# First read of the state-space kernel's H rows moved ahead of two G matrices, and two drains on GpSimd, in a two-block transformer kernel

## The chip, the cores and the metric

The program runs on one core of a Trainium2 chip (trn2). Its engines are called here as the profile calls them: PE (TensorE; PEld is its weight load), DVE (VectorE), ACT (ScalarE), POOL (GpSimd), and SP, which here only issues transfers. The metric is the device time of one execution in microseconds (us), the median of several runs. Lower is better.

## What is computed

Two transformer blocks in a row on 512 tokens of width 1024, all in float32. Block one: a mixer (convolution and dilated attention), cross-attention to 256 memory rows with 4 heads of 256, and a mixture of 32 experts with two per token. Block two: a forgetting attention and a state-space layer (S5) side by side, and again 32 experts, half as wide.

What the change touches is the preparation of the state-space layer of block two, which depends on parameters alone:

```python
A_bar = jnp.exp(A * dt)
B_bar = ((A_bar - 1.0) / A)[..., None] * Bm
Bu = jnp.einsum('bsgc,gpc->bsgp', uf.astype(jnp.complex64), B_bar)
A_seq = jnp.broadcast_to(A_bar, Bu.shape)
_, state = lax.associative_scan(_linear_combine, (A_seq, Bu), axis=1)
Cm = lax.complex(C_re.astype(f32), C_im.astype(f32))
y = jnp.real(jnp.einsum('gcp,bsgp->bsgc', Cm, state))
```

The kernel runs the recurrence in chunks of 8 tokens with matrices made beforehand: G (powers of A_bar times B_bar, into the state), H (C times powers of A_bar, out of the state), and K = B_bar by H, the response inside a chunk, written to DRAM as the triangular matrices T.

## The kernel before

One instruction stream per engine is written out by hand, and semaphores tie them. An engine works strictly in the order written; a `wait_ge` holds everything behind it on its engine.

The stages around the change, by their place in the profiled execution:

- Until about 405 us POOL computes eight H pieces (`s5_matrices_pool`, L1157 to L1166) and writes them to the DRAM tensor `ssm_h` (L1171). Beside this PE works on block one.
- POOL then makes four G matrix pieces (u = 0 to 3, L1185 to L1199), each followed by `g_ready` + 1. DVE makes the other four (`s5_late_dve`, L1229 to L1236), each followed by `g_late` + 1. POOL's temporaries `G_tmp` lie in `work[:, 2048:3072]`, DVE's in `work[:, 1024:2048]`.
- After its four pieces POOL reads H rows back for the K product: for each quad q = 0 to 3 two transfers (L1209) into `Hq`, which lies over both of those temporaries, `work[:, 1024:3072]`. Hence the first read stands behind all of POOL's pieces and behind `g_late` 4. The read for q waits for `k_done` q, the K product before it.
- PE meanwhile computes the queries of the cross-attention (L278) and enters its loop over 16 (head, tile) pairs (`xattn_pe`). In each pass it does scores (L278), four transposes of one G piece (`s5_turn_pe`, L1247) and the transposes of the probabilities (L1316). In every fourth pass (n = 3, 7, 11, 15) it waits for the H rows (`hq_in`) and does the K product of quad n // 4: 8 matmuls, 16 in the profile (L1256); then come the matmuls by the values (L278). In these passes PE's later work stands behind `hq_in`.
- Passes 0 to 3 use the G pieces u = 0 and 1, passes 4 to 7 u = 2 and 3 (POOL's), passes 8 to 15 DVE's.
- DVE copies each K product into `KS` (L1270, L1271), in `work[:, 5120:6144]`, where B_bar and C, which POOL's G pieces read, lie too. Once all four stand there, POOL writes T (L1213).
- SP loads the first two expert matrices when the queries no longer need their places, and waits for T to be written (`t_out`, L2143) before the third.

Then come block one's output projection and experts, the entry of block two (`entry_pool` on POOL, L2386), the state-space layer, attention, and the second expert stage. There `moe_pool` (m = 9) adds each expert's rows into the output with an indirect transfer (L2095): for expert e it waits for `yready`; the buffer `yb` has four places, so ACT's scaling for expert e (L2022) waits for the add of expert e - 4 to have landed.

```python
pool.wait_ge(S("g_late"), 4)
pool.wait_ge(S("tab_out"), 32)
for q in range(4):
    if q:
        pool.wait_ge(S("k_done"), q)
    for c in range(2):
        pool.dma_start(Hq[:, :, c, :], by_quad(Hm)[:, q, :, 288 * c:288 * c + 256]).then_inc(S("hq_in"), 16)
```

Of the kernel before, what the change touches and what calls it, by code (L numbers as in the profile page):

```python
# [190 lines left out]
def build(nc, a, out):  # L191
    es = ExitStack()
    with es:
# [13 lines left out]
        def since(name):  # L207

            return SHARED.get(name, (name, 0))[1]
# [798 lines left out]
        G_tmp = work[:, 2048:3072].rearrange("p (a f e n) -> p a f e n", a=4, f=2, e=8)  # L1008
        G_tmp_late = work[:, 1024:2048].rearrange("p (a f e n) -> p a f e n", a=4, f=2, e=8)
        B_tmp = spare[:, 5376:6400].rearrange("p (a i n) -> p a i n", a=4, n=16)  # L1010
        Hq = work[:, 1024:3072].rearrange("p (f c n) -> p f c n", f=4, c=2)
        KS = work[:, 5120:6144].rearrange("p (q n) -> p q n", q=4)

        def G_of(n):
# [104 lines left out]
        def s5_matrices_pool(pool):  # L1119
            done = [0]  # L1120

            def op(ins):
                ins.then_inc(S("pool_chain"), 1)
                done[0] += 1

            def settle():
                pool.wait_ge(S("pool_chain"), done[0])

            tt = nc.gpsimd.tensor_tensor
            halves = (slice(0, 64), slice(64, P))  # L1130
            after_stage(pool, 2)
            pool.dma_start(raw_bc, a["ssm_bc"]).then_inc(S("bc_in"), 16)
            op(nc.gpsimd.memset(spare[:, 3072:5376], 0.0))
            op(nc.gpsimd.memset(spare[:, 7168:8192], 0.0))
            pool.wait_ge(S("sp_done"), 1)
            pool.wait_ge(S("bc_in"), 16)
            kr, ki = (sc[:, i, :].unsqueeze(2).to_broadcast([P, SS, 16]) for i in (12, 13))
            op(tt(B_tmp[:, 0], B_bar[:, 0], kr, ALU.mult))
            op(tt(B_tmp[:, 1], B_bar[:, 1], ki, ALU.mult))
            op(tt(B_tmp[:, 2], B_bar[:, 1], kr, ALU.mult))  # L1140
            op(tt(B_tmp[:, 3], B_bar[:, 0], ki, ALU.mult))
            settle()
            op(tt(B_bar[:, 0], B_tmp[:, 0], B_tmp[:, 1], ALU.subtract))
            op(tt(B_bar[:, 1], B_tmp[:, 2], B_tmp[:, 3], ALU.add))
            settle()
            for c in range(2):
                for h, r in enumerate(halves):
                    op(nc.gpsimd.tensor_copy(B_mask[r, c, :, h, :], B_bar[r, c]))
            settle()
            for u in range(8):  # L1150
                Q, f0 = u // 2, 2 * (u % 2)
                sh = [P, 2, 9, 16]
                cr, ci = (by_quad(C_raw[:, c])[:, Q, f0:f0 + 2, :].unsqueeze(2).to_broadcast(sh) for c in range(2))
                are, nai = (w.rearrange("p e (f q) -> p q f e", q=4)[:, Q, f0:f0 + 2, :].unsqueeze(3).to_broadcast(sh)
                            for w in (pw[:, 0], nim))
                settle()
                op(tt(H_tmp[:, 0], cr, are, ALU.mult))  # L1157
                op(tt(H_tmp[:, 1], ci, nai, ALU.mult))
                op(tt(H_tmp[:, 2], cr, nai, ALU.mult))
                op(tt(H_tmp[:, 3], ci, are, ALU.mult))  # L1160
                settle()
                if u >= 2:
                    pool.wait_ge(S(f"h_out{u % 2}"), 16 * (u // 2))
                for h, r in enumerate(halves):
                    op(tt(H_buf[r, u % 2, :, 0, :, h, :], H_tmp[r, 0], H_tmp[r, 1], ALU.add))
                    op(tt(H_buf[r, u % 2, :, 1, :, h, :], H_tmp[r, 2], H_tmp[r, 3], ALU.subtract))  # L1166
                    if u == 0 and h == 0:
                        resnorm_pool("n5", 0, 1)
                        pool.wait_ge(S("n5_rstd"), since("n5_rstd") + 1)
                settle()  # L1170
                pool.dma_start(by_quad(Hm)[:, Q, f0:f0 + 2, :],  # L1171
                               spare[:, 3072 + 1152 * (u % 2):4224 + 1152 * (u % 2)].rearrange("p (f n) -> p f n", f=2)
                               ).then_inc(S(f"h_out{u % 2}"), 16)
                if 1 <= u < T:
                    resnorm_pool("n5", u, u + 1)
                if u == T:
                    pool.wait_ge(S("tab_sin"), 2)
                    pool.dma_start(Km[:, 0:2 * SS * CH], work[:, 0:2 * SS * CH]).then_inc(S("tab_out"), 16)
                    pool.dma_start(Km[:, 2 * SS * CH:3 * SS * CH], junk2[:, :]).then_inc(S("tab_out"), 16)

            for b in range(2):
                pool.wait_ge(S(f"h_out{b}"), 16 * 4)
            for u in range(4):
                Q, f0 = u // 2, 2 * (u % 2)
                op(nc.gpsimd.memset(spare[:, 3072 + 1024 * u:4096 + 1024 * u], 0.0))  # L1185
                sh = [P, 2, 8, 16]
                br, bi = (by_quad(B_bar[:, c])[:, Q, f0:f0 + 2, :].unsqueeze(2).to_broadcast(sh) for c in range(2))
                are, aim = (prv[:, c].rearrange("p e (f q) -> p q f e", q=4)[:, Q, f0:f0 + 2, :].unsqueeze(3).to_broadcast(sh)
                            for c in range(2))
                settle()  # L1190
                op(tt(G_tmp[:, 0], br, are, ALU.mult))
                op(tt(G_tmp[:, 1], bi, aim, ALU.mult))
                op(tt(G_tmp[:, 2], br, aim, ALU.mult))
                op(tt(G_tmp[:, 3], bi, are, ALU.mult))
                settle()
                area = spare[:, 3072 + 1024 * u:4096 + 1024 * u].rearrange("p (f c e h n) -> p f c e h n", f=2, c=2, e=8, h=2)
                for h, r in enumerate(halves):
                    op(tt(area[r, :, 0, :, h, :], G_tmp[r, 0], G_tmp[r, 1], ALU.subtract))
                    op(tt(area[r, :, 1, :, h, :], G_tmp[r, 2], G_tmp[r, 3], ALU.add))  # L1199
                settle()  # L1200
                pool.sem_inc(S("g_ready"), 1)

            pool.wait_ge(S("g_late"), 4)
            pool.wait_ge(S("tab_out"), 32)
            for q in range(4):
                if q:
                    pool.wait_ge(S("k_done"), q)
                for c in range(2):
                    pool.dma_start(Hq[:, :, c, :], by_quad(Hm)[:, q, :, 288 * c:288 * c + 256]).then_inc(S("hq_in"), 16)  # L1209
            pool.wait_ge(S("ks_ready"), 8)  # L1210
            pool.wait_ge(S("zeroed"), 16 * (STEPS - 1))
            for s in range(STEPS):
                pool.dma_start(Tm[s // 2, :, :, s % 2, 32 * s:256], KS[:, :, 0:256 - 32 * s]).then_inc(S("t_out"), 16)  # L1213
# [25 lines left out]
        def s5_turn_pe(pe, n):  # L1239
            if n < 8:  # L1240
                pe.wait_ge(S("g_ready"), n // 2 + 1)
            else:
                pe.wait_ge(S("g_late"), n // 2 - 3)
            if n:
                pe.wait_ge(S("gt_out"), n)
            for b in range(4):
                last = nc.tensor.transpose(ps[:, 6, b * P:b * P + P], G_of(n)[:, b * P:b * P + P], ident[:, :])  # L1247
            last.then_inc(S("gt_turned"), 1)
            if n % 4 == 3:
                q = n // 4  # L1250
                pe.wait_ge(S("hq_in"), 32 * (q + 1))
                if q:
                    pe.wait_ge(S("ks_ready"), 2 * q)
                for f in range(4):
                    for c in range(2):
                        last = nc.tensor.matmul(ps[32 * f:32 * f + 32, 7, 0:256],  # L1256
                                                B_mask[:, c, q + 4 * f, :, :].rearrange("p h n -> p (h n)"),
                                                Hq[:, f, c, :], start=c == 0, stop=c == 1)
                last.then_inc(S("k_done"), 1)

        def s5_turned_act(act, n):
# [5 lines left out]

        def s5_kernel_dve(dve, q):
            dve.wait_ge(S("k_done"), q + 1)
            dve.tensor_copy(KS[:, q, 32:256], ps[:, 7, 32:256]).then_inc(S("ks_ready"), 1)  # L1270
            dve.scalar_tensor_tensor(KS[:, q, 0:32], col("eye32", 0, 32), col("ssm_d", q), ps[:, 7, 0:32], ALU.mult,  # L1271
                                     ALU.add).then_inc(S("ks_ready"), 1)
# [790 lines left out]
        def moe_pool(pool, m):  # L2063
# [13 lines left out]
            for e in range(NE):  # L2077
# [3 lines left out]
                add_rows(pool, m, rowdst[:, expert(e):expert(e) + 1], yb[:, e % 4, :]).then_inc(S(f"yadd{m}_{e % NG}"), 16)  # L2081
                if e % 2 == 1 and e // 2 + 4 < NE // 2:
                    gather(e // 2 + 4)
                if e == NE - 8:
                    pool.wait_ge(S(f"planned{m}"), since(f"planned{m}") + 1)
                    pool.wait_ge(S(f"xturned{m}"), since(f"xturned{m}") + NE // 2 - 3)
# [1030 lines left out]
        def _(pool):  # L3117
# [4 lines left out]
            moe_pool(pool, 6)  # L3122
            over_pool(pool, 6)
            entry_pool(pool)
            fox_in_pool(pool)
            fox_pool(pool)
            mix2_pool(pool)
# [103 lines left out]
```

## Time and profile before

| | |
|---|---|
| median of 3 runs | 1804.73 us (1803.51 to 1806.19) |
| the profiled execution: time, span | 1803.88 us, 1802.0 us |
| busy: PE, DVE, ACT, POOL | 89%, 30%, 18%, 22% of the span |
| moved by DMA | 437.16 MB, mean 243 GB/s |
| mean granted TensorE clock | 0.978 of full speed |

The span runs from the first to the last instruction of the profiled execution; its time has 1.88 us more around it. A busy PE is not a PE at its peak, and the share of busy time is an average over stages with different limits. In rows of the profile, [x <-y] is the idle time before an instruction and what ended it; L12 is line 12 of the kernel before. The two expert stages (about 576 to 1054 us and 1535 to 1790 us) stream 32 experts' weights each; between them lies block two's mixer.

### The profile page before, as it was taken

What the parts mean: (1) busy time and instruction counts of PE and PEld (TensorE: products, weight loads), DVE (VectorE), ACT (ScalarE), POOL (GpSimd) and SP (SyncE); (2) the same over time, 40 slices, a digit from 0 to 9 for tenths busy, and PEclk for the clock granted to TensorE, in tenths of its full rate; (3) what the DMA queues carried; (4) which work ended last, traced back from release to release, by engine and by line L of the source; (5) the groups of instructions that cost most, each with busy time, mean ns of one, the idle gap of its engine ahead of it and who ended that gap; (6) DMA issues with size and microseconds to landing.
All of it is one profiled execution on the core that took longest, in us unless ns stands there. A gap on an engine that the chain in (4) does not pass through costs nothing.

```text
span 1802.0 us, 22881 instructions
## 1 busy us (share of the span) xinstructions
PE 1598.7 (89%) x9029; PEld 873.0 (48%) x9029; DVE 539.2 (30%) x1227; ACT 331.9 (18%) x710; POOL 392.2 (22%) x377
## 2 busy tenths in 40 slices
PE   7999999997998999777877759999999998899885
PEld 4445666443545554333343326444444444667553
DVE  3765554742315221001010022614400015321110
ACT  3002453221312000000000030413510003111110
POOL 0121442686101111111111110014201000223222
PEclk9999999999998999999999989999999999999998
DMA  8343111253466999999999977921041265999995
GB/s 310 101 128 118 47 48 59 73 207 140 163 245 232 395 415 414 419 420 415 418 420 418 414 229 210 268 96 47 1 86 56 92 247 208 346 398 397 399 403 202
DMA packets 103480, 437.16 MB, mean 243 GB/s; under 512 B 16249, under 2 KB 23961, under 8 KB 77137
## 3 DMA queue, kind: packets, MB, share of 16 engines
q1 hardware_dynamic: 75888, 387.12, 55.4%
q0 software_dynamic: 18320, 30.76, 6.3%
q10 hardware_dynamic: 9168, 17.84, 2.7%
q8 instruction: 73, 1.20, 0.3%
q14 instruction: 31, 0.25, 0.0%
HBM read 410.98 MB, written 40.65 MB: 251 GB/s over the span
## 4 chain that ended last, share of the span: by engine, by line
PE 58%; DMA 27%; POOL 5%; DVE 4%; issue 2%; ACT 2%; SPq 1%; ACTq 0%; POOLq 0%; DVEq 0%
PE ps L278 23%; DMA ring<-in_w 19%; PE ps L1928 9%; PE ps L1461 5%; DMA ring<-in_w_expert_up 4%; PE ps L1944 4%; PE ps L756 2%; PE ps L2446 2%; PE ps L1447 2%; DMA ring<-in_w_expert_down 1%; PE ps L811 1%; PE ps L844 1%; PE ps L2955 1%; PE ps L761 1%; PE ps L859 1%
## 5 line engine op out<-in xcount | busy, mean ns | idle before, releaser
L1928 PE MATMUL ps<-ring,work 128*64 128x256 f32 (+1 forms) x2784 | 252.5, 330 | 41.7 <-DMA ring<-in_w 29.2
L278 PE MATMUL ps<-kept,ring 128*128 128x512 f32 x592 | 256.1, 593 | 4.3 <-ACT kept L542 1.3
L1928 PEld LDWEIGHTS ps<-ring,work 128*64 128x64 f32 x2784 | 172.4, 137 | 127.1 <-DMA ring<-in_w 48.1
L278 PEld LDWEIGHTS ps<-kept,ring 128*128 128x128 f32 x592 | 111.8, 190 | 145.9 <-issue 142.0
L2056 DVE TENSOR_TENSOR work<-work,ps 128x256 f32<-128x256 f32 (+1 forms) x64 | 22.7, 355 | 496.9 <-PE ps L1928 496.9
L1944 PE MATMUL ps<-ring,work 128*64 128x512 f32 x536 | 125.5, 603 | 32.5 <-DMA ring<-in_w 25.1
L2095 POOL DMA_INDIRECT hres<-work,rowdst x33 | 51.7, 1567 | 403.9 <-ACT work L2022 389.6
L1928 PE MATMUL ps<-kept,work 128*64 128x256 f32 (+1 forms) x1280 | 116.4, 330 | 20.7 <-DMA kept<-in_w 14.8
L278 PE MATMUL ps<-ring,kept 128*128 128x512 f32 (+1 forms) x320 | 125.1, 550 | 0.6 <-PE ps L278 0.6
L1928 PEld LDWEIGHTS ps<-kept,work 128*64 128x64 f32 x1280 | 80.1, 137 | 60.7 <-DMA kept<-in_w 23.5
L2012 ACT ACTIVATE work<-ps 128x256 f32<-128x256 f32 (+1 forms) x64 | 21.1, 330 | 438.5 <-PE ps L1928 438.5
L278 PEld LDWEIGHTS ps<-ring,kept 128*128 128x128 f32 x320 | 60.3, 190 | 63.0 <-issue 61.0
L2095 POOL DMA_INDIRECT out<-work,rowdst x33 | 51.8, 1570 | 171.1 <-ACT work L2022 170.8
L1461 PE MATMUL ps<-ring,kept 128*128 128x512 f32 x192 | 85.2, 595 | 1.0 <-ACTq L257 0.7
L2022 ACT ACTIVATE work<-ps,gslot 128x512 f32<-128x512 f32 x64 | 44.0, 687 | 211.8 <-PE ps L1944 211.8
L1944 PEld LDWEIGHTS ps<-ring,work 128*64 128x64 f32 x536 | 36.7, 138 | 94.4 <-issue 58.1
L1944 PE MATMUL ps<-kept,work 128*64 128x512 f32 x240 | 58.5, 624 | 14.5 <-DMA kept<-in_w 9.5
L1461 PE MATMUL ps<-ring,work 128*128 128x512 f32 x128 | 58.6, 611 | 2.4 <-POOL work L3018 2.2
L1461 PEld LDWEIGHTS ps<-ring,kept 128*128 128x128 f32 x192 | 35.4, 190 | 43.5 <-issue 41.9
L278 PE MATMUL ps<-ring 128*128 128x512 f32 x128 | 55.3, 592 | 0.0
L647 DVE SCALAR_TENSOR_TENSOR ring<-ring,cols 128x512 f32<-128x512 f32 x60 | 54.5, 950 | 0.6
L3011 DVE TENSOR_TENSOR work<-work,ps 128x512 f32<-128x512 f32 x16 | 11.0, 689 | 136.3 <-PE ps L278 136.3
(470 smaller groups left out, 1973.6 us busy)
## 6 DMA issues: line engine op xcount, KB each, us to landing
ring<-in_w SPq DMA_DIRECT2D x65, 2048.0 KB, 42.0
kept<-in_w SPq DMA_DIRECT2D x28, 2048.0 KB, 42.5
ring<-in_w_in SPq DMA_DIRECT2D x13, 2048.0 KB, 14.7
ring<-in_w_expert_down SPq DMA_DIRECT2D x23, 1024.0 KB, 23.4
ring<-in_w_expert_gate SPq DMA_DIRECT2D x22, 1024.0 KB, 20.6
ring<-in_w_expert_up SPq DMA_DIRECT2D x22, 1024.0 KB, 22.4
kept<-in_w_expert_gate SPq DMA_DIRECT2D x10, 1024.0 KB, 23.4
kept<-in_w_expert_down SPq DMA_DIRECT2D x10, 1024.0 KB, 23.9
```

What stands on the lines that cost most here:

```text
L278: last = nc.tensor.matmul(out_, l, r, start=i == 0, stop=i == len(pairs) - 1)
L647: ins = dve.scalar_tensor_tensor(cacc[:, c, :], cpad[:, c, j:j + SEQ], w, cacc[:, c, :], ALU.mult, ALU.add)
L756: last = nc.tensor.matmul(dst.rearrange("p (m n) -> p m n", m=MT), weight(f"w_xk{u // 4}")[:, k, u % 4 * P:u % 4 * P + P], memT[:, :, k, : ...
L1447: last = nc.tensor.matmul(ps[:, t, :], src(k)[:, t * P:t * P + P], weight(nm)[:, k, :], start=k == 2, stop=k == 1)
L1461: last = nc.tensor.matmul(ps[:, b * T + t, :], src(k)[:, t * P:t * P + P], weight(nm)[:, k, :], start=k == 0, stop=k == KD - 1)
L1928: last = nc.tensor.matmul(dst[64 * hf:64 * hf + 64, :], xT[:, k, :], view[:, k * ff + hf * hw:k * ff + hf * hw + hw], start=k == 0, stop=k ...
L1944: last = nc.tensor.matmul(ps[64 * hf:64 * hf + 64, bank, :], hT_[:, i % nch, 64 * (i // nch):64 * (i // nch) + 64], down[:, i, hf * 512:hf ...
L2012: nc.scalar.activation(gb[:, i % 2, 0:hw], ps[:, 0, 0:hw], ACT.Silu).then_inc(S(f"silu{m}"), 1)
L2022: nc.scalar.activation(yb[:, j % 4, :], ps[:, 6 + j % 2, :], ACT.Identity, scale=gslot[:, expert(j):expert(j) + 1]).then_inc(S(f"yready{m} ...
L2056: dve.tensor_tensor(hb[:, i % 2, 0:hw], gb[:, i % 2, 0:hw], ps[:, 1, 0:hw], ALU.mult).then_inc(S(f"hready{m}"), 1)
L2095: return pool.indirect_dma_start(out=by_half(acc(m)), out_offset=bass.IndirectOffsetOnAxis(ap=rows_, axis=0), in_=src, in_offset=None, bou ...
L2446: last = nc.tensor.matmul(ps[64 * q:64 * q + 64, s2, :], hs[:, k, 2 * s2 + q, :], weight("u")[:, k, :], start=k == 0, stop=k == KD - 1)
```

## The change

The H rows get two other places, one for each half c: `spare[:, 1024:2048]` (inside the tile `ring`) and `work[:, 1024:2048]`. The read for q = 0 is issued behind POOL's second G piece (u = 1), ahead of the third and fourth, after waits for `n5_turned`, `g_late` 4 and `tab_out`. The other reads stay behind all four pieces and behind `k_done`. DVE's copy of the first K product waits for `g_ready` 4 besides. POOL gets two `drain()` instructions: one after `entry_pool`, before `fox_in_pool`; one in the second expert stage behind the add of expert 22 (`NE - 10`).

```diff
-        Hq = work[:, 1024:3072].rearrange("p (f c n) -> p f c n", f=4, c=2)
+        Hq = [v.rearrange("p (f n) -> p f n", f=4) for v in (spare[:, 1024:2048], work[:, 1024:2048])]
...
+            def h_rows(q):
+                if not q:
+                    pool.wait_ge(S("n5_turned"), since("n5_turned") + T)
+                    pool.wait_ge(S("g_late"), 4)
+                    pool.wait_ge(S("tab_out"), 32)
+                for c in range(2):
+                    pool.dma_start(Hq[c], by_quad(Hm)[:, q, :, 288 * c:288 * c + 256]).then_inc(S("hq_in"), 16)
...
                 pool.sem_inc(S("g_ready"), 1)
-
-            pool.wait_ge(S("g_late"), 4)
-            pool.wait_ge(S("tab_out"), 32)
-            for q in range(4):
-                if q:
-                    pool.wait_ge(S("k_done"), q)
-                for c in range(2):
-                    pool.dma_start(Hq[:, :, c, :], by_quad(Hm)[:, q, :, 288 * c:288 * c + 256]).then_inc(S("hq_in"), 16)
+                if u == 1:
+                    h_rows(0)
+
+            for q in range(1, 4):
+                pool.wait_ge(S("k_done"), q)
+                h_rows(q)
...
-                                                Hq[:, f, c, :], start=c == 0, stop=c == 1)
+                                                Hq[c][:, f, :], start=c == 0, stop=c == 1)
...
             dve.wait_ge(S("k_done"), q + 1)
+            if not q:
+                dve.wait_ge(S("g_ready"), 4)
...
+                if e == NE - 10 and m == 9:
+                    pool.drain()
...
             entry_pool(pool)
+            pool.drain()
             fox_in_pool(pool)
```

On POOL, at the end of the second G piece, the order before (`ring<-work` are the G pieces, `ssm_h` the H rows in DRAM; waits are named by semaphore):

```order
L1198 TENSOR_TENSOR ring<-work 64x2x8x16
L1199 TENSOR_TENSOR ring<-work 64x2x8x16
L1185 MEMSET ring 128x1024 [waits pool_chain]
L1191 TENSOR_TENSOR work<-work 128x256 [waits pool_chain]
L1192 TENSOR_TENSOR work<-work 128x256
```

and now:

```order
L1206 TENSOR_TENSOR ring<-work 64x2x8x16
L1207 TENSOR_TENSOR ring<-work 64x2x8x16
L1187 DMA ring<-ssm_h 128x4x256 [waits pool_chain,tab_out,g_late,norm_turned]
L1187 DMA work<-ssm_h 128x4x256
L1193 MEMSET ring 128x1024
L1199 TENSOR_TENSOR work<-work 128x256 [waits pool_chain]
L1200 TENSOR_TENSOR work<-work 128x256
```

Two transfers and their waits have come in between the second and the third piece.

On POOL behind the fourth G piece, before:

```order
L1209 DMA work<-ssm_h 128x4x256 [waits pool_chain,tab_out,g_late]
L1209 DMA work<-ssm_h 128x4x256
L1209 DMA work<-ssm_h 128x4x256 [waits k_done]
L1209 DMA work<-ssm_h 128x4x256
L1209 DMA work<-ssm_h 128x4x256 [waits k_done]
L1209 DMA work<-ssm_h 128x4x256
```

and now:

```order
L1187 DMA ring<-ssm_h 128x4x256 [waits pool_chain,k_done]
L1187 DMA work<-ssm_h 128x4x256
L1187 DMA ring<-ssm_h 128x4x256 [waits k_done]
L1187 DMA work<-ssm_h 128x4x256
L1187 DMA ring<-ssm_h 128x4x256 [waits k_done]
L1187 DMA work<-ssm_h 128x4x256
```

The first pair is gone from here; the pairs for q = 1 to 3 are the same transfers at the same place, each half into its own tile.

## Rows read from the trace of the kernel before

**Rows 1.** the page: shares of the chain that ended last, by engine

```profile
PE 58%; DMA 27%; POOL 5%; DVE 4%; issue 2%; ACT 2%; SPq 1%; ACTq 0%; POOLq 0%; DVEq 0%
```

**Rows 2.** the chain in order of time, 400 to 500 us: start, us, what

```profile
433.51 0.80 POOL work L1209
434.31 15.29 DMA work<-ssm_h
```

**Rows 3.** timeline of PE, 440 to 490 us: start, us, what, idle before

```profile
440.55 0.63 PE L1247 MATMUL ps<-ident,ring 128*128 128x128 f32 x4 [0.16 <-ACT ring L1264]
449.65 1.96 PE L1256 MATMUL ps<-work,ring 128*32 128x256 f32 x16 [8.47 <-DMA work<-ssm_h]
...
463.89 1.09 PE L1256 MATMUL ps<-work,ring 128*32 128x256 f32 x16
...
476.16 1.09 PE L1256 MATMUL ps<-work,ring 128*32 128x256 f32 x16
```

**Rows 4.** windows: length; busy PE, PEld, DVE, ACT, POOL; clock, DMA share, GB/s

```profile
420.00:432.00 12.00, 12.00 (x29) 5.13 (x27) 0.00 (x0) 0.60 (x1) 11.38 (x17) 1.00 0.00 0
...
446.00:448.00 2.00, 0.00 (x0) 0.00 (x0) 0.00 (x0) 0.00 (x0) 0.00 (x0) 0.50 0.90 279
```

**Rows 5.** timeline of POOL, 380 to 490 us

```profile
418.95 0.72 POOL L1199 TENSOR_TENSOR ring<-work 64x256 f32<-64x256 f32 x1
...
426.42 0.95 POOL L1185 MEMSET ring<- 128x1024 f32 x1 [0.15 <-POOL ring L1199]
...
432.13 0.73 POOL L1199 TENSOR_TENSOR ring<-work 64x256 f32<-64x256 f32 x1
433.51 1.56 POOL L1209 DMA_DIRECT2D work<-ssm_h  x2 [0.66 <-POOL ring L1199]
```

**Rows 6.** timeline of DVE, 414 to 450 us

```profile
414.11 0.89 DVE L1236 TENSOR_TENSOR kept<-work 64x256 f32<-64x256 f32 x1
```

**Rows 7.** H reads issued after 450 us, then all after 430 us

```profile
DMA to landing us min/median/max: 4.3/4.8/5.4
...
DMA to landing us min/median/max: 4.3/8.5/15.3
```

**Rows 8.** DMA issues, 430 to 434 us: count, KB each, us to landing

```profile
ring<-in_w SPq DMA_DIRECT2D x2, 2048.0 KB, 15.7
work<-ssm_h POOLq DMA_DIRECT2D x1, 512.0 KB, 12.1
```

**Rows 9.** timeline of SP's issues, 420 to 760 us

```profile
432.34 0.81 SPq L2123 DMA_DIRECT2D ring<-in_w  x2
502.07 0.33 SPq L2123 DMA_DIRECT2D work<-in_w  x1
502.49 55.92 SPq L2123 DMA_DIRECT2D ring<-in_w  x4
```

**Rows 10.** SP's waits, 432 to 600 us: total, times, longest

```profile
SPq L2143 <- DMA ssm_t<-work: 68.8, 1, 68.8
```

**Rows 11.** windows, around and in the first expert stage

```profile
540.00:560.00 20.00, 19.04 (x99) 10.15 (x99) 11.03 (x41) 6.90 (x16) 1.36 (x3) 1.00 0.31 114
...
600.00:660.00 60.00, 58.01 (x436) 33.12 (x433) 14.77 (x41) 5.68 (x11) 10.05 (x7) 1.00 1.02 410
```

**Rows 12.** timeline of POOL, entry of block two and second expert stage

```profile
1191.73 5.43 POOL L2796 TENSOR_TENSOR qstat<-qstat,halves 128x32 f32<-128x32 f32 x1 [118.39 <-DVE qstat L2782]
...
1705.50 1.58 POOL L2095 DMA_INDIRECT out<-work,rowdst  x1 [5.51 <-ACT work L2022]
1715.52 1.56 POOL L2095 DMA_INDIRECT out<-work,rowdst  x1 [8.45 <-ACT work L2022]
```

**Rows 13.** timeline of ACT, the scaling for expert 27

```profile
1747.01 0.69 ACT L2022 ACTIVATE work<-ps,gslot 128x512 f32<-128x512 f32 x1 [1.78 <-PE ps L1944]
```

**Rows 14.** DMA issues of the span: the adds, median us to landing

```profile
out<-work,rowdst POOLq DMA_INDIRECT x33, 8.5
```

**Rows 15.** window late in the second expert stage

```profile
1660.00:1780.00 120.00, 98.00 (x1137) 66.38 (x1135) 16.74 (x37) 14.87 (x30) 31.57 (x24) 1.00 1.02 397
```

## The prediction

> **What bounds the kernel now.** I read the shares of the chain first: PE carries 58% of it, transfers 27% [rows 1]. PE is the bound of most stages, and a wait on PE is time of the kernel if everything behind it follows PE. So I looked at the place of the change in the chain in order of time. Ahead of the first K product it does not run through PE at all but through POOL, piece by piece: the issue of the first H rows at 433.51, then 15.29 us of transfer [rows 2]. The timeline of PE shows the other end: PE finishes its fourth G transpose at 440.55 + 0.63 = 441.2, sits idle 8.47 us for the H rows, and starts the K product at 449.65 [rows 3]. The windows show the clock: 1.00, that is 2.4 GHz, in 420 to 432 us, where PE is busy without a break, and 0.50, that is 1.2 GHz, in 446 to 448 us, five us into the idle time [rows 4]. So the first K product takes 1.96 us and the later ones 1.09 [rows 3].
>
> **Part 1, the first H read moves up.** The second G piece of POOL ends at 418.95 + 0.72 = 419.7 us [rows 5]. The moved read waits for three things. The last of DVE's late G pieces ends at 414.11 + 0.89 = 415.0 [rows 6], 4.7 us before POOL asks. `n5_turned` and `tab_out` are what DVE's memset ahead of those pieces waits for too, so both are older still. The two transfers are thus issued from 419.7 to about 421.9. In 420 to 432 us the DMA engines are idle, share 0.00 [rows 4]. The six later H reads land in 4.3 to 5.4 us [rows 7], so I take 5.4: the rows are there by 427.3, 13.9 us before PE asks at 441.2. The 8.47 us are gone.
>
> The clock follows. From K product to K product PE takes 463.89 - 449.65 = 14.24 us in the first round and 476.16 - 463.89 = 12.27 us in the second [rows 3]; both rounds hold the same work. The difference, 1.97 us, is what the low clock cost the first round. Without the idle time nothing in these rows makes PE slower than in the second round, whose rhythm of small gaps ran at 1.00. Saved: 8.47 + 1.97 = 10.44 us. If the clock stayed low for another reason, 8.47 would be left; it can't give more than both.
>
> **Part 2, what stands behind the read on POOL.** The issues of a pair take 1.56 us plus 0.66 us of gap [rows 5]. The third G piece now ends at 426.42 + 2.2 = 428.6, the fourth at 432.13 + 0.73 + 2.2 = 435.1. PE needs the third in its fifth pass, behind the first K product, so after 442.3: 13.7 us of cover. The new wait of DVE's first `KS` copy on `g_ready` 4 is for 435.1, and that copy also waits for the K product at 442.3; behind it on DVE stand the copies of the probabilities, which PE awaits, and they are not held. Both parts cost 0. If the cover went, POOL would have to be 7 us later than reckoned.
>
> **Part 3, the second H read meets the weights.** What is late next is the read for q = 1. It is issued behind the K product, at 441.2 + 1.09 = 442.3, into the transfer of two expert matrices, 4 MB, that SP issued at 432.34. Those took 15.7 us to land, and the first pair of H rows, issued 1.2 and 2 us behind them, 12.1 and 15.3 [rows 8] [rows 7]. In the changed kernel the same bytes are under way up to 450 us: the matrices, one pair of H rows (now q = 1), the G pieces of ACT. All of them had landed at 434.31 + 15.29 = 449.6 [rows 2]. PE asks for q = 1 one round behind the first product, at 441.2 + 12.3 = 453.5. That leaves 3.9 us; I count 0. Whether the read shares or queues is the open point. The rows show sharing: the pair issued behind the matrices landed about with them. The Trainium skill, "DMA: Bandwidth & Descriptors", section "Queues, rings and completion order", says that each transfer engine takes turns between its queues packet by packet. By that rule the read would not stand behind what is left of the matrices; the sum would be the same, and rival A would be rarer than the rows alone make it.
>
> **Part 4, does the saving reach the end?** SP issued its third expert load at 502.07 and the next from 502.49 [rows 9], and it had waited 68.8 us for T to be written [rows 10]. T follows the fourth K product, so this load moves up with PE. The others wait for PE's output projection. In 540 to 560 us the transfers are at a share of 0.31, from 600 us at 1.02 [rows 11]: the saturated stream begins behind work that is itself 10.4 us earlier, and only the two matrices of 432 us, which had landed by 448 us, are not tied to it. The entry of block two, the mixer and the second expert stage each wait for the one before. I pass on all of it.
>
> **Part 5, the drains.** No row shows a drain on POOL. The one at the entry falls into 118.39 us in which POOL is idle [rows 12]; between 0 and 118 us it costs nothing. The one in the second expert stage stands behind the add for expert 22, which ends at 1705.50 + 1.58 = 1707.1; the next add starts at 1715.52 after 8.45 us of idle time [rows 12]. Up to 8.4 us it delays nobody. Beyond that the add for expert 23 is late, which ACT awaits before it scales expert 27, at 1747.01 [rows 13]; the add needs 8.5 us to land [rows 14]. So the drain may last 1747.0 - 8.5 - 1707.1 = 31.4 us before it costs anything. The bounds are 0 and the end of the stage's stream: the DMA share is 1.02 until 1780 us [rows 15], 72.9 us. Nearest to a drain is the issue that it follows, 1.58 us, and I take 0 for the end. A drain frees nothing that another engine awaits, so no gain either. The Trainium skill, "PSUM — Partial Sum Buffer", section "Engine vs sequencer instructions", has a drain wait until its engine is fully idle; by this rule it ends with POOL's own work and the cost is also 0, while a drain that waited for the transfers it had issued would still stay under 31.4.
>
> **The sum.** 10.44 saved and 0 added: the profiled execution's 1803.88 us would be 1793.4. The median of the runs shown is 0.85 above that execution, so the forecast is 1804.73 - 10.44 = **1794.3 us**.
>
> **The rivals.**
> A, a new wait in place of the old: the read for q = 1 takes 15.3 us as its forerunner did, from its second issue at 443.1, and lands at 458.4. PE waits 4.9 us, and the clock falls as before for up to 1.97. Saved 3.6 to 5.5, say 4.2: 1800.5. For it speaks that the load on the queues at the issue is nearly the same; against it that by then 10 of the 15.7 us of the matrices are over. 6%.
> B, the gain is swallowed by the first expert stage, which streams 400 us at the limit of the transfers. 1804.7. It would need the stream's start to be fixed in time; the wait of 68.8 us on T speaks against it. 5%.
> C, slower: the drain in the second expert stage holds POOL until the transfers under way have landed, in a stage in which they don't cease before 1780 us. It costs nothing up to 31.4 us and outweighs the saving from 31.4 + 10.4 = 41.8 us on. At its full 72.9 us it delays expert 27 by 41.5 us: 1794.3 + 41.5 = 1835.8. Against it: the nearest rows of POOL are in single microseconds. 3%.
> D, the change does not do what it says: one of the three waits holds POOL, the read goes out as late as before, and third and fourth G pieces stand behind it. 1804.7. The 4.7 us of margin on `g_late` speak against it. 2%.
>
> **How the numbers follow.** The forecast has the other 84%. A measurement of this kernel can tell about 0.2%, 3.6 us, from no change. Faster: forecast and A, 0.90. Within it: B and D, 0.07. Slower: C, 0.03. The range: at the low end the fastest run shown less the saving, 1803.51 - 10.44, less the 2.7 us by which the runs shown differ, 1790.4; at the high end rival A, 1800.5. It takes in the 8.47 without the clock (1796.3) and leaves out 10%.
>
> **What the profile after would show.** Right: the first pair of H reads issued near 420 us and landed by 428; no idle time of PE for `ssm_h` before the first K product, which starts at about 441.2 and takes 1.1 us; a clock of 1.00 in 442 to 456 us; four K products 12.3 us apart; SP's third expert load at 491.6; the same 10.4 us at every later landmark; POOL's adds from expert 23 on not later than ACT's scalings. Wrong: PE idle for H rows before the second product (A); that load 10 us earlier and the end of the first expert stage not (B); a gap on POOL behind the add for expert 22 that ends at no scaling (C); the first H pair near 433 us (D).

## The result and the profile after

The changed kernel takes **1788.24 us** (median of 4 runs, 1787.69 to 1791.32); the kernel before took 1804.12 us beside it (4 runs, 1803.15 to 1806.19). The ratio is 0.9911, 95% interval 0.9899 to 0.9923: 16 us faster, where 10.4 were forecast. 1788.24 lies 2.2 us below the range, 1790.4 to 1800.5. The profiled execution of the changed kernel took 1791.32 us, its span is 1789.5.

The chain of the page, by engine, against [rows 1]:

```profile
PE 62%; DMA 26%; DVE 4%; ACT 2%; issue 2%; POOL 2%; SPq 1%; ACTq 0%; POOLq 0%; DVEq 0%
```

POOL has fallen from 5% to 2% of it and PE risen from 58% to 62%: ahead of the first K product the chain now runs through PE, as the timelines show.

The first part went as reckoned. The timeline of POOL in the changed kernel, around the moved read (start, us, what, idle before):

```profile
420.34 0.73 POOL L1207 TENSOR_TENSOR ring<-work 64x256 f32<-64x256 f32 x1
421.75 0.80 POOL L1187 DMA_DIRECT2D ring<-ssm_h  x1 [0.69 <-POOL ring L1207]
422.55 0.75 POOL L1187 DMA_DIRECT2D work<-ssm_h  x1
...
435.64 0.73 POOL L1207 TENSOR_TENSOR ring<-work 64x256 f32<-64x256 f32 x1
443.96 0.78 POOL L1187 DMA_DIRECT2D ring<-ssm_h  x1 [7.58 <-PE ps L1262]
```

The first pair of H rows goes out at 421.75, not 433.51 [rows 5]; the profiled execution as a whole is 1.4 us later here than the one before, and was so ahead of the change (PE's passes begin at 434.33 where they began at 432.93). The pair for q = 1 waits 7.58 us for the first K product and for nothing else. The issues of 419 to 423 us, us to landing:

```profile
ring<-ssm_h POOLq DMA_DIRECT2D x1, 512.0 KB, 4.4
work<-ssm_h POOLq DMA_DIRECT2D x1, 512.0 KB, 5.7
```

The second of the pair, issued at 422.55, is there by 428.3. PE's timeline:

```profile
441.95 0.63 PE L1253 MATMUL ps<-ident,ring 128*128 128x128 f32 x4 [0.16 <-ACT ring L1270]
442.51 0.66 PE L1262 MATMUL ps<-ring 128*32 128x256 f32 x8
442.96 0.64 PE L1262 MATMUL ps<-work,ring 128*32 128x256 f32 x8
...
454.78 0.66 PE L1262 MATMUL ps<-ring 128*32 128x256 f32 x8
...
467.06 0.66 PE L1262 MATMUL ps<-ring 128*32 128x256 f32 x8
...
479.34 0.66 PE L1262 MATMUL ps<-ring 128*32 128x256 f32 x8
```

No idle time stands ahead of the first K product, where there were 8.47 us [rows 3]. The products are 12.27, 12.28 and 12.28 us apart. The clock is 1.00 (2.4 GHz) where it had been 0.50 [rows 4]:

```profile
442.00:456.00 14.00, 12.87 (x86) 8.30 (x87) 6.61 (x22) 6.40 (x17) 1.54 (x2) 1.00 0.83 304
446.00:448.00 2.00, 1.03 (x4) 0.44 (x3) 1.56 (x6) 0.74 (x2) 0.00 (x0) 1.00 0.80 293
```

SP's third expert load stood at 502.07 [rows 9] and is now 9.17 us earlier, 10.6 against the start of PE's passes:

```profile
492.90 0.33 SPq L2133 DMA_DIRECT2D work<-in_w  x1
```

The other 5 to 6 us come from a place that the forecast does not have. The last transfer that POOL issues adds the rows of the overflow round to the output. Timeline of POOL, the kernel before (span 1802.0):

```profile
1788.39 1.58 POOL L2095 DMA_INDIRECT out<-work,tokcol  x1 [5.49 <-ACT work L2234]
```

and the changed kernel (span 1789.5):

```profile
1781.48 1.58 POOL L2105 DMA_INDIRECT out<-work,tokcol  x1 [5.48 <-ACT work L2244]
```

The add comes 6.91 us earlier, the end of the span 12.5. From the end of that add to the end of the span, called the tail from here on, it was 12.03 us and is now 6.44. (Spans are printed to a tenth, so every tail below is good to 0.05 us.) No timeline has an instruction of POOL in that stretch, since timelines leave control instructions out. The view of one line has them: line 193 is the end of the program. The kernel before, first (durations in ns min/median/max, first and last start in us):

```profile
L193 POOLq DRAIN  x1: 6814/6814/6814, 1795.0 to 1795.0; - x1
L193 SPq DRAIN  x1: 13/13/13, 1768.4 to 1768.4; - x1
L193 ACTq DRAIN  x1: 8/8/8, 1795.4 to 1795.4; - x1
L193 DVEq DRAIN  x1: 10/10/10, 1795.4 to 1795.4; - x1
L193 PEldq DRAIN  x1: 8/8/8, 1795.5 to 1795.5; - x1
```

The changed kernel:

```profile
L193 POOLq DRAIN  x1: 1200/1200/1200, 1788.1 to 1788.1; - x1
L193 SPq DRAIN  x1: 13/13/13, 1761.5 to 1761.5; - x1
L193 ACTq DRAIN  x1: 8/8/8, 1788.5 to 1788.5; - x1
L193 DVEq DRAIN  x1: 66/66/66, 1788.8 to 1788.8; - x1
L193 PEldq DRAIN  x1: 8/8/8, 1788.6 to 1788.6; - x1
```

Every engine closes with a drain that the source does not write. POOL's took 6.81 us and is the last thing that happens but for 0.2 us of semaphores; now it takes 1.20. The difference, 5.61 us, is the whole of what the tail lost (5.59). The added drains themselves, the entry's and the expert stage's:

```profile
L3135 POOLq DRAIN  x1: 6017/6017/6017, 1066.0 to 1066.0; - x1
L2093 POOLq DRAIN  x1: 10696/10696/10696, 1698.3 to 1698.3; - x1
```

They are not short: 6.02 and 10.70 us. The first runs out at 1072.0, long before POOL's next operation, and the second ends at 1709.0. Timeline of POOL behind the first and around the second, against [rows 12]:

```profile
1184.89 5.43 POOL L2806 TENSOR_TENSOR qstat<-qstat,halves 128x32 f32<-128x32 f32 x1 [118.16 <-DVE qstat L2792]
...
1698.54 1.58 POOL L2105 DMA_INDIRECT out<-work,rowdst  x1 [5.53 <-ACT work L2030]
1710.19 1.56 POOL L2105 DMA_INDIRECT out<-work,rowdst  x1 [10.07 <-PE ps L1927]
1715.76 1.60 POOL L2105 DMA_INDIRECT out<-work,rowdst  x1 [2.63 <-ACT work L2030]
```

and of ACT, the scaling for expert 27, against [rows 13]:

```profile
1740.06 0.69 ACT L2030 ACTIVATE work<-ps,gslot 128x512 f32<-128x512 f32 x1 [1.81 <-PE ps L1952]
```

### The profile page after: what moved, and what is told of

It reads as the page before. It is cut to its first block, busy times and chain, and to the rows that moved or that the text cites. A ratio compares the mean times of both kernels' runs of the same rounds, so it can differ in the third digit from the quotient of the medians.

```text
span 1789.5 us, 22884 instructions
## 1 busy us (share of the span) xinstructions
PE 1600.4 (89%) x9029; PEld 875.2 (49%) x9029; DVE 539.4 (30%) x1227; ACT 331.9 (19%) x710; POOL 391.5 (22%) x377
## 4 chain that ended last, share of the span: by engine, by line
PE 62%; DMA 26%; DVE 4%; ACT 2%; issue 2%; POOL 2%; SPq 1%; ACTq 0%; POOLq 0%; DVEq 0%
PE ps L278 27%; DMA ring<-in_w 19%; PE ps L1936 9%; PE ps L1469 5%; DMA ring<-in_w_expert_up 4%; PE ps L1952 4%; PE ps L756 2%; PE ps L2456 2%; PE ps L761 2%; PE ps L1455 2%; DMA ring<-in_w_expert_down 1%; PE ps L811 1%; PE ps L844 1%; PE ps L2965 1%; PE ps L859 1%
## 5 line engine op out<-in xcount | busy, mean ns | idle before, releaser
L1952 PE MATMUL ps<-ring,work 128*64 128x512 f32 x536 | 129.2, 618 | 33.1 <-DMA ring<-in_w 25.0
L1952 PE MATMUL ps<-kept,work 128*64 128x512 f32 x240 | 55.5, 597 | 14.7 <-DMA kept<-in_w 10.4
```

The costliest lines, as they stand in the source:

```text
L1952: last = nc.tensor.matmul(ps[64 * hf:64 * hf + 64, bank, :], hT_[:, i % nch, 64 * (i // nch):64 * (i // nch) + 64], down[:, i, hf * 512:hf ...
```

## The experiments

The first four were made when the closing drain had not been looked at; what was known was that the saving was 6 us too large and that it sat behind the last add.

**The read alone.** The change without both drains.

```diff
-                if e == NE - 10 and m == 9:
-                    pool.drain()
...
-            pool.drain()
```

> The moved H read without either drain. Seen so far: the changed kernel is 15.9 us faster by its median, 12.5 by its span; in the profile the stretch from the end of POOL's last add to the end of the span is 12.0 us before and 6.4 after, and an instruction fetch falls into it before. Theory P (place in the code: the drains move the last instructions of POOL against the blocks in which its code is fetched): 10.4 us faster than before, tail of 12.0 us as before. Theory R (the extra 5.5 us belong to the moved read or to chance in the transfer-bound stages; the drains do nothing): 16 us faster, tail of 6.4. Theory Q (a drain does something where it stands): 10.4, and the tail could be either.

Measured: 1794.66 us (1791.92 to 1795.69, 5 runs), ratio 0.9941, interval 0.9928 to 0.9954. Against the 1805.54 of the kernel before beside it that is 10.9 us, and against the forecast 1794.3 it is 0.4 off. The tail is 12.06 us, as before. What was forecast is what the read does.

**The drains alone.** The kernel before with both drains.

```diff
+                if e == NE - 10 and m == 9:
+                    pool.drain()
...
+            pool.drain()
```

> The kernel before with both drains and the H read where it was. P: 5.6 us faster than before, tail of 6.4 us, the 8.5 us wait of PE for the H rows unchanged. R: no difference, tail of 12.0. Q: 5.6 us faster, and the time is gained near 1707 us, behind the drain, not in the tail.

Measured: 1801.45 us (1797.36 to 1803.35, 7 runs), ratio 0.9971, interval 0.996 to 0.9983, so 5.2 us faster by the ratio and 4.1 by the medians: clear of no change. The tail is 6.44 us, that of the change, though the last add of its profiled execution comes at 1793.48, later than before. PE still waits 8.32 us for the H rows. The shares add up, 0.9941 times 0.9971 is 0.9912. Theory R is out.

**The read and one drain,** first the one at the entry, then the one in the expert stage.

```diff
             entry_pool(pool)
+            pool.drain()
```

> Moved read and the drain at the entry of block two alone. P: this drain and the other are worth the same, one instruction each: e3 and e4 come out alike, both 10.4 us faster than before if one instruction is too little to move the end, both 16 if one suffices. Q: 10.4, if the drain of the expert stage is the one that counts. R: 16.

```diff
+                if e == NE - 10 and m == 9:
+                    pool.drain()
```

> Moved read and the drain in expert stage two alone. P: the same as e3. Q: 16 us faster, unlike e3. R: 16.

Measured: entry 1793.0 us (1789.39 to 1795.15, 6 runs), ratio 0.9931, interval 0.9919 to 0.9943, tail 9.62 us; expert stage 1788.7 us (1787.13 to 1789.59, 5 runs), ratio 0.9906, interval 0.9893 to 0.9919, tail 6.41. One drain is as good as two if it is the later one, and the earlier gives less than half. That is neither Theory P, by which the two are alike, nor Theory Q, whose gain would lie right behind the drain. In the view of line 193 the closing drains are:

```profile
L193 POOLq DRAIN  x1: 4397/4397/4397, 1785.5 to 1785.5; - x1
```

```profile
L193 POOLq DRAIN  x1: 1201/1201/1201, 1786.3 to 1786.3; - x1
```

Counted in the trace, 132 transfers of POOL stand ahead of the closing drain in the kernel before, 53 behind the entry drain, 14 behind that of the expert stage. (The record of that drain begins 0.2 us ahead of the row of the add that stands before it in the program; counted by start times this add falls behind the drain. The expectations below count so: 15 behind that drain, 39 with 24 more transfers, 38 ahead of it, and 14 up to a drain in the overflow round. In the order of the program it is 14, 38, 39 and 13.) 4.40 / 53 = 0.083 and 1.20 / 14 = 0.086 us. Hence a new theory, B: a drain works off what POOL's transfers have left behind since the last one. Its rival is again the place of the code.

With the expert-stage drain alone 118 transfers stand ahead of it, and it takes 12.79 us instead of 10.70; the kernel is no slower for that.

**Two drains at the entry.**

```diff
             entry_pool(pool)
             pool.drain()
+            pool.drain()
```

with the one in the expert stage left out.

> The read as in the change, both drains in a row at the entry of block two, none in expert stage two: as many POOL instructions ahead of the end as in the change. What the records of the closing drain (line 193, POOL) show so far: 6.81 us without an added drain (132 POOL transfers issued since the start), 4.40 us with the entry drain alone (53 issued since), 1.20 us in both kernels with the expert-stage drain (15 issued since). Theory B, backlog: POOL's closing drain works off what its transfers left behind since its last drain, about 0.083 us for each. Then the second entry drain takes under 0.2 us, the closing one 4.40, and the stretch from the last add's end to the end of the span is 9.6 us. Theory P, place: what counts is where the closing code lies, so how many instructions stand ahead of it. Then two drains at the entry do what the two of the change do: closing drain 1.2 us, stretch 6.4.

Measured: 1793.08 us (one run), tail 9.67.

```profile
L3133 POOLq DRAIN  x1: 6017/6017/6017, 1065.5 to 1065.5; - x1
```

```profile
L3134 POOLq DRAIN  x1: 47/47/47, 1071.5 to 1071.5; - x1
```

```profile
L193 POOLq DRAIN  x1: 4391/4391/4391, 1786.6 to 1786.6; - x1
```

Theory P falls: two drains at the entry leave the closing drain where one leaves it. The second, right behind the first, costs 0.047 us, so an instruction of this kind is not long in itself.

**More transfers behind the last drain.**

```diff
                 if e == NE - 10 and m == 9:
                     pool.drain()
+                if e >= NE - 8 and m == 9:
+                    for i in range(3):
+                        at = 16 * (3 * (e - NE + 8) + i)
+                        pool.dma_start(Gm[:, at:at + 16], ident[:, 0:16]).then_inc(S("filler"), 16)
+                    pool.wait_ge(S("filler"), 48 * (e - NE + 9))
```

> The change, and behind each of the last eight adds of expert stage two three more small transfers issued by POOL (128 rows of 16 numbers into a scratch tensor that nothing reads), 24 in all, behind the last drain. Theory B, backlog: 15 + 24 = 39 transfers stand behind the last drain, so the closing drain takes 39 * 0.083 = 3.2 us instead of 1.20, and the stretch behind the last add is 8.5 us. If only indirect transfers count it stays at 1.20. Theory P, place: anything, without relation to the count.

```profile
L193 POOLq DRAIN  x1: 3160/3160/3160, 1799.9 to 1799.9; - x1
```

3.16 us for 38 transfers. The 24 more cost 1.96 us, 0.082 each: the forecast of 3.2 holds, and plain transfers count like indirect ones. (Both kinds have 128 rows here, so these runs don't tell whether transfers or their rows are counted.) The tail is 7.97, less than the 8.5 expected, since POOL was at its closing drain 4.6 us behind the last add and not 5.0. The kernel itself takes 1805.13 us (one run): the wait for the three fillers holds POOL about 8 us behind each of the first five adds and 2 us behind the last three, which is the edit's doing and no matter here.

**More compute behind the last drain.** The same with small copies.

```diff
+                if e >= NE - 8 and m == 9:
+                    for i in range(3):
+                        at = 16 * (3 * (e - NE + 8) + i)
+                        nc.gpsimd.tensor_copy(junk[:, at:at + 16], ident[:, 0:16])
```

> The change, and behind each of the last eight adds of expert stage two three small POOL copies (128 by 16 numbers into a scratch tile) in place of the three transfers of the run before: 24 more compute instructions behind the last drain. Theory B as the last runs left it (closing drain = 0.081 us for each POOL transfer since the last drain: 15 give 1.20, 39 gave 3.16, 53 gave 4.40): compute leaves nothing behind, the closing drain stays at 1.20 us and the stretch behind the last add at 6.4. Theory C, every POOL instruction leaves something: it grows, to as much as 3.2 us.

Measured: closing drain 1.200 us, tail 6.47, 1789.32 us (one run). Transfers alone leave something behind. Theory C falls.

**Is there a cap?** The read alone, with the 24 fillers, no drain.

> The read of the change, no added drain, and the 24 more transfers of the run with more transfers: 156 POOL transfers stand behind no drain but the closing one, where 132 took 6.81 us. Theory B with a cap (132 at 0.083 would be 10.9, not 6.81; 79 took 6.02): what a drain works off is bounded, the closing drain takes 6.81 us again. Theory B without a cap, with cheaper transfers of the first block: 24 more at 0.081 make it 8.8 us.

```profile
L193 POOLq DRAIN  x1: 6814/6814/6814, 1795.9 to 1795.9; - x1
```

156 transfers take what 132 took, to the nanosecond (the kernel takes 1804.79 us, one run, with the waits for the fillers in it). So what a drain works off is bounded, and the bound is reached by 132. With 79 it was 6.02 (the entry drain), which is 0.5 less than 79 times 0.082: either the bend begins below 79, or block one's transfers, other ones than these, cost less. Nor do these runs show what is full.

**What does a drain cost that nothing covers?** One behind every add of expert stage two.

```diff
-                if e == NE - 10 and m == 9:
+                if m == 9:
                     pool.drain()
```

> The change with its expert-stage drain made 32: one behind every expert's add in stage two. It prices a drain that nothing covers. In the change that one drain's record is 10.70 us long, begins with the add ahead of it, and the next add is issued 11.65 us after the one before, against 9.10 us in the kernel with the entry drain alone. 38 transfers at 0.083 us are 3.2 us of it. Theory B, backlog alone: each of the 32 drains has 1 or 2 transfers behind it, so a record of under 2 us (the add's own 1.6 us in it), adds come as far apart as before (5.5 to 9 us), and the time stays within 1 us of the change's, with a closing drain of 1.20. Theory L, a drain also waits until POOL's transfers in flight have landed (8.5 us for an add): each record is 8 to 10 us long, adds are at least 9 to 10 us apart instead of 6.2 us on average in the first 20, and the kernel is 40 to 90 us slower.

Measured: 1843.71 us (1840.86 to 1845.38, 4 runs), ratio 1.0216, interval 1.02 to 1.0231, 55 us slower than the change. The view of the drain's line, and POOL's timeline:

```profile
L2093 POOLq DRAIN  x32: 3527/8082/14321, 1545.3 to 1826.6; - x32
```

```profile
1641.28 1.56 POOL L2105 DMA_INDIRECT out<-work,rowdst  x1 [8.52 <-ACT work L2030]
1643.15 1.06 POOL L2078 DMA_INDIRECT work<-hmid,rowtok  x1 [0.30 <-issue]
1653.24 1.58 POOL L2105 DMA_INDIRECT out<-work,rowdst  x1 [9.03 <-issue]
1664.03 1.56 POOL L2105 DMA_INDIRECT out<-work,rowdst  x1 [9.21 <-ACT work L2030]
```

With one or two transfers ahead of it a drain still takes 8.08 us in the median, while the adds that this kernel issues up to 1790 us take 8.3 us from issue to landing. The landings themselves show what it waits for. One drain begins at 1653.02 and ends at 1663.18; the add, issued at 1653.24, landed 9.87 us later, at 1663.11. The views of the two lines at that place, the drain first:

```profile
L2093 POOLq DRAIN  x1: 10162/10162/10162, 1653.0 to 1653.0; - x1
```

```profile
DMA to landing us min/median/max: 9.9/9.9/9.9
```

The one before stands behind an add and a gather; the gather, issued at 1643.15, landed at 1652.27 and the drain ended at 1652.38, 2.9 us behind the add's landing. Of the 32 drains, 31 end 0.07 to 0.12 us behind the landing of the last transfer ahead of them, the first 0.30 us. From the first add to the twentieth it is 200.3 us (1545.56 to 1745.87) instead of 127.7 (1545.83 to 1673.55) in the change, where adds are 6.7 us apart and not 6.2 as the expectation has it. The closing drain takes 0.216 us here, with two transfers behind the last of the 32 (the 1.20 of the expectation belongs to 14). So a drain does two things: it works off the backlog, and it waits until POOL's transfers in flight have landed. How the two go together is open: the drain behind expert 22 in the change ends 1.65 us behind the landing of its add, neither 0.07 nor the 3.2 of 39 transfers. Theory L holds, and with it the mechanism of rival C; only its price was wrong, since one drain waits for POOL's own transfers and not for SP's stream.

**A third drain,** in the overflow round, where POOL waits 5.48 us for the last scaled rows.

```diff
+                    if m == 9:
+                        pool.drain()
                     pool.wait_ge(S(f"over{m}_yready"), b + 2)
```

> The change with a third drain: in the overflow round of expert stage two, behind the gather and ahead of POOL's wait for the last scaled rows, where POOL sits idle for 5.48 us. Theory B, backlog: one transfer is issued behind it, so the closing drain falls from 1.20 us to about 0.1, and the stretch behind the last add from 6.44 to 5.3 to 5.4 us; the third drain itself has 14 transfers to work off (about 1.2 us, or until the gather just issued has landed, 2.2 us) and stays inside the idle time, so the kernel is 1.1 us faster than the change. Theory L, a drain also waits for the transfers in flight: the same, as only the gather is in flight. Theory P, place: one more instruction, no forecast below 1.2 us. If the last add is issued later than in the change by more than 0.3 us against the last gather, the drain was not covered.

Measured: 1789.6 us (1786.57 to 1790.99, 5 runs), ratio 0.9916, interval 0.9903 to 0.993. The third drain takes 1.61 us and is covered, since the last add is issued 6.56 us behind the last gather, where it was 6.55. The closing drain falls as said, but the tail only to 6.15 us, not to 5.3:

```profile
L193 POOLq DRAIN  x1: 123/123/123, 1786.3 to 1786.3; - x1
L193 DVEq DRAIN  x1: 66/66/66, 1787.1 to 1787.1; - x1
```

POOL is done at 1786.4 and the span ends at 1787.4: between them stand the closing steps of the other engines, DVE's last. They begin when ACT and PE have stepped through their own skipped rounds of the overflow loop; in the change ACT's last one ends at 1788.15, as POOL comes to its closing drain (1788.1):

```profile
L2235 ACTq COMPARE_BRANCH  x30: 40/45/54, 1046.3 to 1788.1; - x30
```

So 0.3 us of the 1.08 come out, too little for the measurement.

**The entry and the overflow drain,** without the one in the expert stage, and **the change again** beside it.

> The read of the change, the drain at the entry of block two, and the third drain of the earlier run (overflow round of expert stage two, ahead of POOL's wait for the last scaled rows), without the drain behind expert 22. The overflow drain has 52 transfers to work off, 52 * 0.083 = 4.3 us, in an idle time of 5.48 us, so it is just covered. The closing drain is 0.12 us and the stretch behind the last add 6.15 us, 0.3 less than in the change. The drain behind expert 22 put the next add 11.65 us behind its predecessor against 9.10: if that late add costs something (from the first load of expert stage two to the last add: 338.4, 339.0 and 339.4 us with that drain and the read, 337.1, 337.7 and 337.8 without), this kernel gives it back: 1 to 1.5 us faster than the change in all. If the late add costs nothing: 0.3 us faster, which 5 rounds cannot tell from none. If the overflow drain is not covered, the last add comes more than 6.56 us behind the last gather.

> The change as it is, again, for the runs beside it: ratio to the kernel before 0.991, expert drain 10.7 us, closing drain 1.20, stretch behind the last add 6.44. From the first load of expert stage two to the last add: 338.4 us if the scatter of that stage is small, 337 to 339.5 if it is as large as the runs so far allow.

Measured: 1790.38 us (1789.27 to 1790.87, 4 runs), ratio 0.9912, interval 0.9895 to 0.9928, and the change 1788.77 (1787.2 to 1789.4, 4 runs), ratio 0.9902, interval 0.9886 to 0.9919. The change has 10.58 and 1.20 us in its expert-stage and closing drains and a tail of 6.4, as expected. In the other kernel the overflow drain takes 4.32 us for 52 transfers, the last add is issued 6.57 us behind the last gather, the tail is 6.10. From the first load of expert stage two to the last add this kernel takes 339.2 us, the change this time 337.6 and the first time 338.4. The same kernel differs by 0.8 us from one time to the next, and the one without the late add takes longest. So the 1 to 1.5 us that the late add seemed to cost are not seen. Of all kernels tried none beats the change; with the expert-stage drain alone (1788.7) it is as fast.

## Why the prediction was wrong

**Part 1** is right to a tenth: no idle time ahead of the first K product, a clock of 1.00, and the last K product at 479.34 where it stood at 488.44, 9.1 us and the 1.4 of the late start: 10.5 us against 10.44. Moved alone, the read gives 10.6 us by the ratio and 10.9 by the medians.

**Part 2** holds. The fourth G piece ends at 435.64 + 0.73 = 436.4 us, ahead of the first K product (442.5), so neither the copy of DVE nor PE waits for it.

**Part 3** holds, with less room than reckoned. The q = 1 pair, issued at 443.96 and 444.74, landed 7.6 and 8.7 us later:

```profile
ring<-ssm_h POOLq DMA_DIRECT2D x1, 512.0 KB, 7.6
work<-ssm_h POOLq DMA_DIRECT2D x1, 512.0 KB, 8.7
```

That is 453.4, and PE asks at 454.8. Rival A, with 15.3 us, did not come. The margin was 1.4 us and not the 3.9 that I gave it: the rows came later than 449.6, the time that I took from the kernel before. The packets show why. There the first packet of the pair moved at 437.87, 4.4 us behind the issue, and from then on its packets went between those of the matrices, whose last began at 447.90: the two shared. Now the first packet of the q = 1 pair moves at 448.28, 4.3 us behind the issue, and the matrices' last begins at 447.86: nothing was left to share, and the changed kernel does not test the sharing that I reckoned with. The q = 0 pair, issued at 421.75 while the transfer engines were idle, had its first packet after 1.5 us. What holds the first packet back in the other two cases is open.

**Part 4** holds within what one execution can say. The 9.17 us at SP's third load are 6.91 at the last add of the first profiled execution and 8.86 at that of the second (1779.53). The first expert stage gives and takes some 2 us from one execution to the next (from that load to the reading back of `hres` it is 555.8 us in the kernel before and 555.4 to 558.0 in the twelve executions with the read); by the medians nothing is lost. Rival B is out, and D too. That the two profiled executions differ by 12.5 us where the medians differ by 15.9 is this scatter.

**Part 5 failed,** with the sentence "A drain frees nothing that another engine awaits, so no gain either", and ahead of it with "No row shows a drain on POOL". One did: the closing drain, 6814 ns, in the view of line 193. I had looked for the end of the kernel in timelines, where the last row of POOL was at 1788.39 in a span of 1802.0, and did not ask what the 12.03 us behind it were. What a drain saves is work of a later drain, and the last one of POOL lies at the end of the program with nothing beside it. The term that the sum put at nothing is 6.81 - 1.20 = 5.61 us; with it the forecast would be 1794.29 - 5.61 = 1788.7 us, against 1788.24 measured.

The same part was wrong on the length as well. I took the row of an issue, 1.58 us, as nearest; the drain behind expert 22 is 10.70 us long. Its next add is issued 11.65 us behind its predecessor, where with the entry drain alone it is 9.10. It cost nothing all the same, for the reason given there: ACT needs that add only for expert 27, whose scaling starts at 1740.06, 21 us after the add had landed (1718.85). Of the rule I had cited from the Trainium skill, "PSUM — Partial Sum Buffer", section "Engine vs sequencer instructions", that a drain waits for its engine to go fully idle, the traces show that for POOL idle takes in its transfers: in the run with 32 drains they end when the last transfer ahead of them has landed.

The Trainium skill, "VectorE: DVE Perf Modes", section "The DRAIN you can't avoid", calls the drains that the runtime puts around a program about 12 ns long on all five engines. For SP, ACT, DVE and PE the trace of the kernel before about agrees (13, 8, 10 and 8 ns; in the changed kernel DVE's is 66). For POOL it is 6814 ns with 132 transfers ahead of it; here the measurement decides.

## What to carry to other kernels

Look at what stands between the last piece of work and the end of the span, in the view that shows control instructions: a kernel that issues many transfers from POOL pays for them once more in the closing drain, up to 6.8 us here. A drain in an idle stretch of POOL late in the program takes that over, if the stretch is long enough for the transfers in flight to land and for 0.08 us per transfer; one is enough. Put behind every add, where POOL is needed again within the landing time of its own transfers, 32 of them cost 55 us here.

## What the runs showed of the hardware

- With nothing in flight POOL's drain takes 0.047 us and 0.082 us more for each transfer that POOL issued since its last drain: 0.047 us for none, 0.12 for 1, 0.22 for 2, 1.20 for 14, 3.16 for 38, 4.40 for 53 (and 4.32 for 52, where a gather was still in flight and landed first). Above, it stays under that line: 6.02 us for 79, 6.81 for 132 and for 156. 24 compute instructions added nothing. That this is a backlog being worked off is the reading that fits; what the drain does in that time no run shows.
- It also waits for the transfers in flight: 31 of 32 drains end 0.07 to 0.12 us behind the last landing. With 39 transfers ahead of it, which by count is 3.2 us, it took 10.4 to 10.7 us right behind an add that needs 8.8 us to land, and 12.8 us with 118.
- The clock of PE was 1.00 throughout 442 to 456 us once the idle time of 8.47 us was gone, and the 1.97 us of the slow round went with it.
- Behind the last add POOL steps through the rounds of the overflow loop that are skipped, and is at the closing drain 5.0 us later: in the kernel before from 1789.97 to 1795.0, in the changed one from 1783.06 to 1788.1. That is most of what is left of the tail, and no run here tried to shorten it. ACT and PE step through their rounds until 1788.2 too, so it would have to shrink on all three: taking 1.08 us from POOL's end alone gave 0.3.
